# A hybrid decoder layer on one core: the prompt's mLSTM state kept over convolved inputs, a product moved to GpSimd, masks announced by halves

## The chip, the cores and the metric
The kernel runs on one core of one Trainium2 chip. The metric is the device time of one execution in microseconds, and the median of the runs counts.

## What is computed
One layer for a prompt of 1024 tokens and for 8 sample tokens that carry states: an input projection, a causal convolution, an SSD scan (16 heads) and an mLSTM scan (4 heads of 256) over chunks of 128 tokens, an output projection with a layer norm, and a product-key expert layer (PEER) that gathers 128 rows of u and v per token. The part that the change touches is the mLSTM of the prompt, with u_c the convolved input:

```
q = u_c @ w_mq;  k = u_c @ w_mk * DK**-0.5          # per head, 256 x 256
att = (q k^T) * exp(dmat - m_t);  num = att @ v + w_inter * (q @ c);  den = att.sum + w_inter * (q @ n)
c_new = w_old * c + (w_s * k)^T v;   n_new = w_old * n + (w_s * k).sum
```

The prompt begins with zero states, and c and n after the last chunk are outputs (p_c, p_n).

## The kernel before
Everything is in one program with semaphores set by hand; each engine has its own written-out order. There are three stages with a barrier between them.

1. **Projections** (to 559 us): TensorE makes channels and tokens from x in split precision, GpSimd splits the weights (L549, L551), VectorE convolves (L633, L635). ScalarE stores token products in DRAM (tok_d, L496) and waits at the end of the stage for all stores, s_ts among them.
2. **Scan** (560 to 856 us, `build_scan`): eight chunks. In each, TensorE transposes the chunk's rows and channels (L978 to L985), makes k and then q from cht and the weights wmk and wmq (L995), transposes k (L1002), makes the scores (L1007), turns the previous chunk's mix (L829), and does the intra-chunk SSD product (L1017: L by xdt), the products with the SSD state (L1024, L1034), one sample's row (L970), q by the state cst (L1043), attention by v (L1049) and the new state (L1053, L1057). ScalarE copies cols, btok and xtok (L1113 to L1115), takes exponentials of L head by head (L1138) with the copies of kT (at head 2) and qT (at head 10) between them. GpSimd adds the causal mask to L (L789), makes e_de and e_ws (L1208, L1209), dx (L1215), xdec (L1218), og (L1221) and scales hT (L1223). VectorE ends the previous chunk with its head norm (L796 to L808), the scaling (L811) and the mix (L814, L816), and then does xdt (L1273), kw (L1276) and the two halves of L by the score mask (L1279). While VectorE works on its norm, ScalarE takes the root in two small activations (L821, L823). Two samples' states are worked in beside it.
   SyncE's loads stand in one queue: v, states and, behind the previous mix, zo; then rows and rb of the next chunk, and cht once L1024 has read the old one. At the end ScalarE stores p_c and p_n, the last mixT, and mixs, the samples' mix, and waits for all of them.
3. **Experts** (856 us to the end, `build_peer`): 656 slots t, with one gathered row of u per slot on VectorE (L2009), rows of v 20 slots later on TensorE (L2388), and the norms, scores and picks of later token tiles spread over the slots by hand. Scores of the first tile are copied by ScalarE (L2120); VectorE picks from them in slots 1 to 22.

The rotating pair of PSUM views is `two(b)`, banks b and b+1. `free(engine, semaphore, n)` is a wait for n that is left out at n = 0.

Of the kernel before, what the change touches and what calls it, by code (L numbers as in the profile page):

```python
# [7 lines left out]
P = 128  # L8
D = 1024
KD = D // P  # L10
SEQ = 1024
CH = 128
# [76 lines left out]
def build(nc, a, o):  # L89
# [13 lines left out]
    mixt_d = dram("mixt_d", (NPAD // CH, P, 16, CH))  # L103
    bc_d = dram("bc_d", (NSMP, 4, P))
# [3 lines left out]
    with top:  # L108
# [19 lines left out]
        s_pre = nc.alloc_semaphore(name="scan_preloaded")  # L128
        with ExitStack() as ctx:
# [85 lines left out]
            s_ts = [sem(f"tok_stored{i}") for i in range(6)]  # L215
# [16 lines left out]
            with nc.Block() as block:  # L232
# [188 lines left out]
                def _(act):  # L421
# [113 lines left out]
                    for b in range(6):  # L535
                        act.wait_ge(s_ts[b], 16 * 3 * NTB // 2)
# [149 lines left out]
        with ExitStack() as ctx:  # L686
            build_scan(nc, a, o, ctx, sem, PB, ident, two, wo, s_wo, s_pre, pre, wp0, first, wp_d, cht_d, chs_d, ych_d, tok_d, rows_d, rows_s_d, mixt_d)
# [9 lines left out]
def build_scan(nc, a, o, ctx, sem, PB, ident, two, wo, s_wo, s_pre, pre, wp0, first, wp_d, cht_d, chs_d, ych_d, tok_d, rows_d, rows_s_d, mixt_d):  # L697
# [24 lines left out]
    qT, kT = sb("qT", [P, MH * KT, CH]), sb("kT", [P, MH * KT, CH])  # L722
# [5 lines left out]
    def wide(ap, n):  # L728
# [14 lines left out]
    hT, cst, nst = sb("hT", [P, D]), sb("cst", [P, MH * KT, DK + 1]), sb("nst", [P, MH * KT])  # L743
    ysb, yst, sq, og = (sb(n, [P, D]) for n in ("ysb", "yst", "sq", "og"))
# [20 lines left out]
    mte, x1e, _, g1e, b1e = first  # L765

    s = {n: sem("scan_" + n) for n in (
        "w wqk setup mask rows ch rb v zo pe_a pe_b pe_bk act_k pe_kk pe_st pe_tr pe_y pe_ys pe_hn pe_ni pe_nx pe_c1 pe_c2 "
        "act_xt act_small act_l act_qk act_l2 act_mt act_nx pool_l pool_arg pool_xdec pool_dx pool_hs pool_og "
        "dve_xdt dve_kw dve_mm dve_att dve_y dve_ys dve_h dve_num dve_var act_ln act_rs dve_c1 dve_c2 dve_mix "  # L770
        "outs stored passed mt0 x0 mt1 wp0 mix0").split()}
    ss = {n: sem("smp_" + n) for n in (
        "ld zeroed pad z_turned y2 ysum yvar yln yrs qk qkr qkt qkc exp arg nst cur outer c_new num numc den den_kept var ln rs mix turned kept stored").split()}
# [5 lines left out]
    def gate_y(ch, r, z, y):  # L779

        ch.link(V.tensor_tensor(y, y, z, ALU.mult))
        V.tensor_tensor_reduce(out=sq[0:r, :], in0=y, in1=y, scale=1.0 / D, scalar=EPS,
# [70 lines left out]
    with nc.Block() as block:  # L853
        @block.sync
        def _(sp):
            for i, q in pairs():
# [6 lines left out]
                if i == 0:  # L863
# [4 lines left out]
                    sp.sem_inc(s["wqk"], 32)  # L868
# [17 lines left out]
                free(sp, s["pe_c2"], i)  # L886
                for j in range(2):
# [53 lines left out]
        def _(pe):  # L941
# [31 lines left out]

            for i, q in pairs():
# [13 lines left out]
                if i == 0:  # L988
                    pe.wait_ge(s["setup"], 1)
                    pe.wait_ge(s["wqk"], 32)  # L990
# [1552 lines left out]
```

## Time and profile before

| | |
|---|---|
| median of 3 runs | 3362.64 us (3362.37 to 3376.76) |
| profiled execution | 3381.35 us, span 3379.5 us |
| mean granted TensorE clock | 0.969 of full |
| busy, share of the span | TensorE 92%, VectorE 75%, GpSimd 51%, ScalarE 28% |
| the scan stage | 560.4 to 855.98 us, chunks of about 31.6 us |
| HBM | 978.59 MB read, 93.11 MB written |

Durations below come from the profiled execution. Durations of TensorE overlap, so its pitch is read from one start to the next. An entry with "x8" sums eight instructions.

### The profile page before, as it was taken

The page shows a single profiled execution, that of the slowest core. Times are in us where ns is not written, and L with a number is a line of the kernel's source. Part 1 is how long each engine was busy: PE and PEld are TensorE (multiplying, and loading weights), DVE is VectorE, ACT ScalarE, POOL GpSimd, SP SyncE. Part 2 cuts the span into 40 slices and gives each one's busy share as a digit, 9 for nine tenths or more (in the row PEclk, how much of TensorE's full clock was granted, in tenths as well). Part 3 has the DMA queues.
Part 4 walks back from the last instruction along what each step waited for, and adds up shares of the span by engine and source line. Part 5 has one row for each costly group of instructions (what it writes and reads, how often), then busy time and mean ns, then how long its engine had stood idle before and what let it go on. Part 6 is the DMA issues. An engine that isn't in the chain of part 4 may idle for free.

```text
span 3379.5 us, 42480 instructions
## 1 busy us (share of the span) xinstructions
PE 3094.6 (92%) x13799; PEld 2052.6 (61%) x13799; DVE 2544.3 (75%) x5370; ACT 937.0 (28%) x2145; POOL 1709.5 (51%) x1418
## 2 busy tenths in 40 slices
PE   9999998999888888988877658999999999999998
PEld 9998887887333233322244336777677766677775
DVE  7771053887678888898899977777777777777777
ACT  3122222655011121111288771111111111111112
POOL 3232131442136666676654555555555555555554
PEclk9999999999999999999989789999999999999999
DMA  4435465778669999999989899999999999999997
GB/s 152 105 84 185 167 211 211 242 260 314 210 204 355 376 360 355 364 374 364 349 315 352 337 361 390 393 384 396 376 406 396 370 383 381 390 399 388 393 394 271
DMA packets 388784, 1074.52 MB, mean 318 GB/s; under 512 B 58824, under 2 KB 148744, under 8 KB 382176
## 3 DMA queue, kind: packets, MB, share of 16 engines
q0 software_dynamic: 186624, 679.56, 53.3%
q1 hardware_dynamic: 151280, 311.91, 26.0%
q10 hardware_dynamic: 50672, 80.51, 6.5%
q8 instruction: 102, 1.67, 0.2%
q14 instruction: 106, 0.87, 0.1%
HBM read 978.59 MB, written 93.11 MB: 317 GB/s over the span
## 4 chain that ended last, share of the span: by engine, by line
PE 40%; DVE 12%; DMA 9%; issue 8%; POOL 4%; ACT 1%; another core or an unknown queue 0%; POOLq 0%; DVEq 0%; SPq 0%; ACTq 0%; PEldq 0%
PE PB L2361 18%; PE PB L2348 14%; DMA vbf<-in_peer_v,gixv 4%; DVE ub L2009 4%; PE PB L2337 3%; DMA x1d<-in_peer_u 3%; PE PB L2388 2%; PE PB L2324 2%; POOL vbf L1737 2%; POOL ub L1737 2%; DMA ub<-in_peer_u,gix 1%; DVE ohb L1956 1%; PE PB L2306 1%; DVE oha L1954 1%; DMA vbf<-in_peer_v,gix 1%
## 5 line engine op out<-in xcount | busy, mean ns | idle before, releaser
L1737 POOL DMA_INDIRECT ub<-in_peer_u,gix x640 | 693.9, 1084 | 713.2 <-DVE hid L2009 507.6
L2361 PE MATMUL PB<-vbd,wd 128*128 128x512 f32 x1536 | 682.6, 594 | 0.0
L2348 PE MATMUL PB<-xds,uts 128*128 128x384 f32 x3072 | 569.4, 340 | 0.0
L2348 PEld LDWEIGHTS PB<-xds,uts 128*128 128x128 f32 x3072 | 531.7, 189 | 0.5 <-issue 0.5
L1737 POOL DMA_INDIRECT vbf<-in_peer_v,gix x340 | 398.6, 1172 | 160.5 <-issue 100.6
L2361 PEld LDWEIGHTS PB<-vbd,wd 128*128 128x128 f32 x1536 | 283.2, 191 | 308.1 <-issue 308.1
L2388 PE MATMUL PB<-vbf,dg 128*64 128x512 f32 x1200 | 320.7, 658 | 113.1 <-DMA vbf<-in_peer_v,gixv 94.5
L1737 POOL DMA_INDIRECT vbf<-in_peer_v,gixv x300 | 323.2, 1077 | 172.5 <-issue 88.5
L1970 DVE TENSOR_TENSOR uts<-PB,uts 128x512 fp32r<-128x512 f32 x256 | 175.6, 686 | 295.7 <-ACT uts L2183 284.0
L2009 DVE CUSTOM_DVE_ANT_0 ub<-ub,x1g 128x1024 f32<-128x1024 f32 x257 | 313.0, 1221 | 51.5 <-DMA ub<-in_peer_u,gix 33.0
L2183 ACT CAST uts<-PB 128x512 fp32r<-128x512 f32 x256 | 149.9, 586 | 642.0 <-PE PB L2337 594.6
L2009 DVE CUSTOM_DVE_ANT_0 ub<-ub,x1gb 128x1024 f32<-128x1024 f32 x256 | 313.0, 1223 | 5.2 <-DMA ub<-in_peer_u,gix 5.0
L2050 DVE SCALAR_TENSOR_TENSOR acc<-vbf,wg,acc 128x1024 f32<-128x1024 f32 x212 | 271.1, 1279 | 5.9 <-DMA vbf<-in_peer_v,gix 4.6
L2388 PEld LDWEIGHTS PB<-vbf,dg 128*64 128x64 f32 x1200 | 85.6, 147 | 298.3 <-issue 272.0
L2306 PE MATMUL PB<-wo,mt 128*128 128x512 f32 x512 | 243.2, 619 | 15.2 <-DVE x L1800 14.8
L2324 PE MATMUL PB<-wp,x1T 128*128 128x512 f32 x432 | 198.6, 602 | 0.0
L2306 PEld LDWEIGHTS PB<-wo,mt 128*128 128x128 f32 x512 | 95.6, 196 | 162.8 <-issue 162.8
L2188 ACT ACTIVATE hg<-PB 128x384 f32<-128x384 f32 x128 | 62.7, 490 | 465.2 <-PE PB L2348 465.2
L2432 PE MATMUL PB<-oha,ohb 128*128 128x128 f32 x768 | 119.1, 309 | 78.7 <-DVE ohb L1956 61.1
L2009 DVE CUSTOM_DVE_ANT_0 ub<-ub,acc 128x1024 f32<-128x1024 f32 x128 | 155.3, 1225 | 32.9 <-DMA ub<-in_peer_u,gix 17.1
L2432 PEld LDWEIGHTS PB<-oha,ohb 128*128 128x128 f32 x768 | 106.0, 214 | 118.8 <-DVE ohb L1956 87.7
L2213 ACT ACTIVATE dg<-fold,wgv 128x64 f32<-128x64 f32 x300 | 87.5, 340 | 324.7 <-PE PB L2388 169.3
(427 smaller groups left out, 5099.0 us busy)
## 6 DMA issues: line engine op xcount, KB each, us to landing
vbd<-in_peer_v SPq DMA_DIRECT2D x128, 512.0 KB
x1d<-in_peer_u SPq DMA_DIRECT2D x96, 512.0 KB
gd_d<-stag ACTq DMA_DIRECT2D x12, 2048.0 KB
gbd<-gd_d SPq DMA_DIRECT2D x16, 1536.0 KB
ubd<-in_peer_u SPq DMA_DIRECT2D x32, 512.0 KB
wtr<-in_w_tok SPq DMA_DIRECT2D x6, 2048.0 KB
tok_d<-stg ACTq DMA_DIRECT2D x48, 256.0 KB, 2.0
rb_e<-rows_d SPq DMA_DIRECT2D x8, 1536.0 KB, 10.5
```

The lines of the kernel that those rows point to most:

```text
L1737: pool.indirect_dma_start(out=buf, out_offset=None, in_=a[table], in_offset=bass.IndirectOffsetOnAxis(ap=index, axis=0)).then_inc(done, 16)
L1970: V.tensor_tensor(uts[:, b % 2, 1, 4 * x:4 * x + 4, :].rearrange("p k e -> p (k e)"), PB[:, 7, :], uts[:, b % 2, 0, 4 * x:4 * x + 4, :].re ...
L2009: V.tensor_tensor_reduce(out=ub[:, t % NB, :], in0=ub[:, t % NB, :], in1=by, scale=1.0, scalar=0.0, op0=ALU.mult, op1=ALU.add, accum_out=i ...
L2050: V.scalar_tensor_tensor(y, vbf[:, v % NB, :], wg[:, hv % 2, col:col + 1], y, ALU.mult, ALU.add, accum_out=total).then_inc(s["ax"], 1)
L2183: S.copy(uts[:, b % 2, 0, 4 * x:4 * x + 4, :].rearrange("p k e -> p (k e)"), PB[:, 7, :]).then_inc(s["utc"], 1)
L2306: last = T.matmul(PB[:, 2 + h, :], mt[:, m % 2, j % 4, :], wo[:, j, h * 512:(h + 1) * 512], start=j == 0, stop=j == 15)
L2324: last = T.matmul(PB[:, 4 + n, :].rearrange("p (h n) -> p h n", h=4), x1T[:, kk, :], wp[:, 4 * n:4 * n + 4, kk, :] if n else wp0[:, :, kk, :],
L2337: last = T.transpose(PB[:, 7, j * P:(j + 1) * P], ubd[b % 4][:, (4 * x + j) * P:(4 * x + j + 1) * P], ident[:, :])
L2348: last = T.matmul(PB[:, 6, 0:TD], uts[:, b % 2, ul, k, :], xds[:, xl, k, :], start=(k, n) == (0, 0), stop=(k, n) == (KD - 1, 2))
L2361: last = T.matmul(PB[:, 2 * d + n, :], wd[:, b % 2, d * CH:(d + 1) * CH], vbd[b % 8][:, n * 512:(n + 1) * 512], start=b == 0, stop=b == NB ...
L2388: last = T.matmul(PB[64 * g:64 * g + 64, x, :], dg[:, n % 2, g, :], vbf[:, (v0 + g) % NB, x * 512:(x + 1) * 512], start=v0 % CH == 0, stop ...
L2432: last = T.matmul(PB[:, 2 + m % 2, :].rearrange("p (b t) -> p b t", t=4)[:, :, x], ohb[:, m % 2, x, :], oha[:, m % 2, x, :], start=True, s ...
```

## The change
For the prompt, the keys are no longer made. Before chunk 0 TensorE turns both weights (32 transposes), and makes per head the product of w_mk and w_mq over their inner dimension, which VectorE keeps with the factor DK**-0.5 in mu0 and mu1. In each chunk one product with it takes the place of the q and k products; its result is scored against the convolved inputs themselves (cht), these are transposed instead of kT, and the state cst is kept over them. The final state (with its sum column) is stored as it is in cu_d; in slots 3 and 6 of the expert stage TensorE multiplies it by w_mk, ScalarE scales it in slots 5 and 7 and stores p_c and p_n, and the first gather of v waits for these stores. Besides: xdt is made by GpSimd, ahead of dx and xdec; exponentials and masks of L are announced by halves; VectorE's memsets are in another order; token stores are awaited by those who need them in the scan, and the mixs store by the first v index loads of the expert stage. The scratch tiles sq, kT and nst are gone.

```diff
+    cu_d = dram("cu_d", (P, MH * KT, DK + 1))
...
+        def tokens_stored(eng):
+
+            for b in range(6):
+                eng.wait_ge(s_ts[b], 16 * 3 * NTB // 2)
+
...
-                    for b in range(6):
-                        act.wait_ge(s_ts[b], 16 * 3 * NTB // 2)
...
+                if i == 0:
+                    tokens_stored(sp)
...
+            def weight_product(h):
+                pe.wait_ge(s["wk_kept"], h + 1)
+                pe.wait_ge(s["wq_kept"], h + 1)
+                for d in range(KT):
+                    for e in range(KT):
+                        last = T.matmul(PB[:, 4 + h, d * DK:(d + 1) * DK], wqT[:, h, e, d * P:(d + 1) * P], wkT[:, h, e, :],
+                                        start=e == 0, stop=e == KT - 1)
+                last.then_inc(s["m_made"], 1)
+
+            pe.wait_ge(s_pre, 80)
+            for h in range(MH):
+                for w, bank in ((wmk, 4 + h), (wmq, h)):
+                    for k in range(KT):
+                        for e in range(KT):
+                            last = T.transpose(PB[:, bank, e * DK + k * P:e * DK + (k + 1) * P], w[:, h, k, e * P:(e + 1) * P], ident[:, :])
+                    last.then_inc(s["w_turned"], 1)
+            weight_product(0)
+            weight_product(1)
+            pe.wait_ge(s["wq_kept"], MH)
...
                 if i == 0:
-                    pe.wait_ge(s["setup"], 1)
-                    pe.wait_ge(s["wqk"], 32)
-                for w, b, done in ((wmk, 6, "pe_bk"), (wmq, 4, "pe_b")):
-                    for h in range(MH):
-                        for e in range(KT):
-                            for k in range(KT):
-                                last = T.matmul(two(b)[:, (h * KT + e) * CH:(h * KT + e + 1) * CH],
-                                                w[:, h, k, e * P:(e + 1) * P], cht[:, UT0 + h * KT + k, :],
-                                                start=k == 0, stop=k == KT - 1)
-                    last.then_inc(s[done], 1)
-                pe.wait_ge(s["act_k"], i + 1)
+                    weight_product(2)
+                    weight_product(3)
+                for h in range(MH):
+                    if i == 0:
+                        pe.wait_ge(s["m_kept"], h + 1)
+                    for e in range(KT):
+                        for k in range(KT):
+                            last = T.matmul(two(4)[:, (h * KT + e) * CH:(h * KT + e + 1) * CH],
+                                            mu(h)[:, k, e * P:(e + 1) * P], cht[:, UT0 + h * KT + k, :],
+                                            start=k == 0, stop=k == KT - 1)
+                last.then_inc(s["pe_b"], 1)
+                pe.wait_ge(s["act_xt"], i + 1)
                 pe.sem_inc(s["passed"], 1)
                 for j in range(MH * KT):
-                    last = T.transpose(two(0)[:, j * P:(j + 1) * P], kT[:, j, :], ident[:, :])
+                    last = T.transpose(two(0)[:, j * P:(j + 1) * P], cht[:, UT0 + j, :], ident[:, :])
...
-                        last = T.matmul(PB[:, 2, h * CH:(h + 1) * CH], kT[:, h * KT + k, :], qT[:, h * KT + k, :],
+                        last = T.matmul(PB[:, 2, h * CH:(h + 1) * CH], cht[:, UT0 + h * KT + k, :], qT[:, h * KT + k, :],
...
-                pe.wait_ge(s["dve_mm"], i + 1)
                 pe.wait_ge(s["dve_kw"], i + 1)
+                pe.wait_ge(s["pool_xdt"], i + 1)
                 for h in range(NH):
+                    if h % 8 == 0:
+                        pe.wait_ge(s["dve_mm"], 2 * i + h // 8 + 1)
...
                     if h == 2:
-                        act.wait_ge(s["pe_bk"], i + 1)
-                        free(act, s["pe_st"], i)
-                        S.activation(kT[:, :, :].rearrange("p a n -> p (a n)"), two(6), ACT.Copy, scale=DK ** -0.5).then_inc(s["act_k"], 1)
-                    if h == 10:
                         act.wait_ge(s["pe_b"], i + 1)
                         free(act, s["pe_nx"], i)
                         S.copy(qT[:, :, :].rearrange("p a n -> p (a n)"), two(4)).then_inc(s["act_qk"], 1)
...
-                last.then_inc(s["act_l"], 1)
+                    if h % 8 == 7:
+                        last.then_inc(s["act_l"], 1)
...
-            S.copy(nst[:, :].unsqueeze(2), cst[:, :, DK:DK + 1]).then_inc(ss["nst"], 1)
-            act.dma_start(o["p_c"], cst[:, :, 0:DK]).then_inc(s["outs"], 16)
-            act.wait_ge(ss["nst"], 1)
-            act.dma_start(o["p_n"], nst[:, :]).then_inc(s["outs"], 16)
+            act.dma_start(cu_d, cst[:, :, :]).then_inc(s["outs"], 16)
...
-            act.wait_ge(ss["stored"], 16)
...
-                    pool.wait_ge(s["setup"], 1)
-                pool.wait_ge(s["dve_xdt"], i + 1)
+                free(pool, s["pe_y"], i)
+                G.tensor_tensor(heads(xdt[:, :], HD), heads(xtok[:, :], HD), wide(cols[q][:, R_DT:R_DT + NH], HD), ALU.mult).then_inc(s["pool_xdt"], 1)
                 free(pool, s["dve_y"], i)
                 G.tensor_tensor(heads(dx[:, :], HD), heads(xtok[:, :], HD), wide(dsk[:, :], HD), ALU.mult).then_inc(s["pool_dx"], 1)
                 pool.wait_ge(s["act_small"], i + 1)
+                pool.wait_ge(s["pool_xdt"], i + 1)
...
+            def keep_turned(h):
+                dve.wait_ge(s["w_turned"], 2 * h + 1)
+                V.tensor_copy(wkT[:, h, :, :].rearrange("p e d -> p (e d)"), PB[:, 4 + h, :]).then_inc(s["wk_kept"], 1)
+
+            def keep_product(h):
+                dve.wait_ge(s["m_made"], h + 1)
+                V.tensor_scalar(mu(h).rearrange("p k e -> p (k e)"), PB[:, 4 + h, :], DK ** -0.5, None, ALU.mult).then_inc(s["m_kept"], 1)
...
-                dve.wait_ge(s["act_xt"], i + 1)
-                free(dve, s["pe_y"], i)
-                free(dve, s["pool_xdec"], i)
-                V.tensor_tensor(heads(xdt[:, :], HD), heads(xtok[:, :], HD), wide(cols[q][:, R_DT:R_DT + NH], HD), ALU.mult).then_inc(s["dve_xdt"], 1)
...
-                dve.wait_ge(s["act_l"], i + 1)
                 for g in range(NG):
-                    last = V.tensor_tensor(L[:, g * 8:g * 8 + 8, :], L[:, g * 8:g * 8 + 8, :],
-                                           PB[:, 3, g * CH:(g + 1) * CH].unsqueeze(1).to_broadcast([P, 8, CH]), ALU.mult)
-                last.then_inc(s["dve_mm"], 1)
+                    dve.wait_ge(s["act_l"], 2 * i + g + 1)
+                    V.tensor_tensor(L[:, g * 8:g * 8 + 8, :], L[:, g * 8:g * 8 + 8, :],
+                                    PB[:, 3, g * CH:(g + 1) * CH].unsqueeze(1).to_broadcast([P, 8, CH]), ALU.mult).then_inc(s["dve_mm"], 1)
...
                 def load_first_gixv(part):
+                    if part == 0:
+                        sp.wait_ge(s_mixs, 16)
...
                 load_mt(2, 0)
+                sp.wait_ge(s["iota"], 1)
+                for n in range(2):
+                    sp.dma_start(wk[n], a["w_mk"][:, 2 * n:2 * n + 2, :, :]).then_inc(s["cul"], 16)
+                sp.dma_start(cu, cu_d).then_inc(s["cul"], 16)
...
                 def gather_v(v):
+                    if v == 0:
+                        pool.wait_ge(s["c_out"], 32)
...
+                    if t in (5, 7):
+                        n = (t - 5) // 2
+                        act.wait_ge(s["c_made"], n + 1)
+                        for b in range(2):
+                            S.activation(cu[:, 4 * n + 2 * b:4 * n + 2 * b + 2, :], PB[:, 4 * b:4 * b + 2, 0:DK + 1], ACT.Copy, scale=DK ** -0.5).then_inc(s["c_kept"], 1)
+                        if n:
+                            act.wait_ge(s["c_kept"], 4)
+                            act.dma_start(o["p_c"], cu[:, :, 0:DK]).then_inc(s["c_out"], 16)
+                            S.copy(nu.unsqueeze(2), cu[:, :, DK:DK + 1]).then_inc(s["c_kept"], 1)
+                            act.wait_ge(s["c_kept"], 5)
+                            act.dma_start(o["p_n"], nu).then_inc(s["c_out"], 16)
...
+                    if t in (3, 6):
+                        n = t // 6
+                        if n == 0:
+                            pe.wait_ge(s["cul"], 48)
+                            pe.wait_ge(s["scc"], 2)
+                        else:
+                            pe.wait_ge(s["c_kept"], 2)
+                        for j in range(4):
+                            h, e, bank = 2 * n + j // 2, j % 2, (0, 1, 4, 5)[j]
+                            for k in range(KT):
+                                last = T.matmul(PB[:, bank, 0:DK + 1], wk[n][:, j // 2, k, e * P:(e + 1) * P], cu[:, h * KT + k, :],
+                                                start=k == 0, stop=k == KT - 1)
+                        last.then_inc(s["c_made"], 1)
+                    if t == 9:
+                        pe.wait_ge(s["c_kept"], 4)
```

## Rows read from the trace of the kernel before

**Rows 1.** Busy time in two stretches; columns: stretch, length, busy (instructions), PEclk, DMA share, GB/s.
```profile
599.70:789.40 189.70, 186.25 (x1388) 158.66 (x1387) 162.69 (x243) 119.66 (x326) 86.59 (x43) 1.00 0.77 265
892.00:2460.00 1568.00, 1330.71 (x4866) 688.24 (x4865) 1318.13 (x3605) 484.39 (x1195) 933.85 (x850) 0.94 0.95 353
```

**Rows 2.** Timeline of chunk 3, all engines: start, duration, engine, line, output<-inputs.
```profile
662.94 0.26 PE L978 MATMUL PB<-ident,rows_e 48*128 48x48 f32 x1
...
664.72 3.74 PE L995 MATMUL PB<-cht_e,wmk_e 128*128 128x128 f32 x32
...
666.58 0.20 POOL L1209 TENSOR_TENSOR e_ws<-cols,rb_e 128x4 f32<-128x4 f32 x1
...
666.85 0.17 DVE L803 TENSOR_TENSOR rs<-mv,den 128x4 f32<-128x4 f32 x1
...
667.74 0.17 DVE L808 TENSOR_TENSOR rs<-rs,den 128x4 f32<-128x4 f32 x1 [0.51 <-ACT rs L823]
...
668.29 3.74 PE L995 MATMUL PB<-cht_e,wmq_e 128*128 128x128 f32 x32
...
669.41 2.44 ACT L1138 ACTIVATE L<-L,cols 128x128 f32<-128x128 f32 x8
670.56 1.22 DVE L816 TENSOR_TENSOR mix<-num,og 128x1024 f32<-128x1024 f32 x1
671.69 1.22 DVE L1273 TENSOR_TENSOR xdt<-xtok,cols 128x1024 f32<-128x1024 f32 x1
...
672.99 1.90 POOL L1215 TENSOR_TENSOR dx<-xtok,dsk 128x1024 f32<-128x1024 f32 x1 [6.21 <-DVE xdt L1273]
...
674.87 2.35 DVE L1279 TENSOR_TENSOR L<-L,PB 128x1024 f32<-128x1024 f32 x2 [0.63 <-ACT L L1138]
...
675.02 1.91 PE L829 MATMUL PB<-ident,mix 128*128 128x128 f32 x16
...
677.28 3.79 PE L1017 MATMUL PB<-xdt,L 128*128 128x64 f32 x32 [0.34 <-DVE L L1279]
...
685.58 3.64 PE L1043 MATMUL PB<-cst,qT 128*128 128x257 f32 x16
...
694.55 0.26 PE L978 MATMUL PB<-ident,rows_e 48*128 48x48 f32 x1
```

**Rows 3.** Timeline of the first stage, VectorE and GpSimd working at once.
```profile
229.09 4.07 POOL L549 CAST wtkh<-wtr 128x4096 fp32r<-128x4096 f32 x1
...
229.61 3.57 DVE L633 TENSOR_SCALAR cv<-xps,cw 128x8 f32<-128x8 f32 x1
...
233.22 10.12 DVE L635 SCALAR_TENSOR_TENSOR cv<-xp,cw,cv 128x1024 f32<-128x1024 f32 x1
233.24 9.02 POOL L551 TENSOR_TENSOR wtkl<-wtr,wtkh 128x4096 fp32r<-128x4096 f32 x1
```

**Rows 4.** Busy time of TensorE just ahead of the scan; columns as named.
```profile
559.00:560.00 1.00, 0.00 (x0) 0.57 0.00 0
```

**Rows 5.** Timeline from the end of the first stage into chunk 0.
```profile
556.53 0.33 ACTq L496 DMA_DIRECT2D tok_d<-stg  x1
...
560.42 0.31 PE L978 MATMUL PB<-ident,rows_e 48*128 48x48 f32 x1 [4.56 <-SPq L865]
...
565.75 5.56 PE L995 MATMUL PB<-cht_e,wmk_e 128*128 128x128 f32 x32 [1.84 <-DVE v L1235]
...
575.98 2.05 PE L1007 MATMUL PB<-qT,kT 128*128 128x128 f32 x16 [0.23 <-ACT qT L1137]
```

**Rows 6.** Timeline at the end of the scan stage.
```profile
835.39 17.33 PE L1065 MATMUL PB<-wo,mt 128*128 128x512 f32 x40
...
843.41 1.08 ACTq L1190 DMA_DIRECT2D mixt_d<-mixs  x1
...
855.98 1.28 ACT L2124 ACT_TABLE_LOAD   x1 [12.60 <-PEq L118]
```

**Rows 7.** Busy time early in the expert stage; columns as in rows 1.
```profile
920.00:930.00 10.00, 3.14 (x4) 1.51 (x5) 9.52 (x40) 0.00 (x0) 2.81 (x3) 0.55 0.54 157
```

More of the change, by code:

```diff
@@ L128, in build @@
         s_pre = nc.alloc_semaphore(name="scan_preloaded")
+        s_ts = [nc.alloc_semaphore(name=f"tok_stored{i}") for i in range(6)]
+        s_mixs = nc.alloc_semaphore(name="smp_mix_stored")
+        def tokens_stored(eng):
+            for b in range(6):
+                eng.wait_ge(s_ts[b], 16 * 3 * NTB // 2)
         with ExitStack() as ctx:
@@ L686, in build @@
         with ExitStack() as ctx:
-            build_scan(nc, a, o, ctx, sem, PB, ident, two, wo, s_wo, s_pre, pre, wp0, first, wp_d, cht_d, chs_d, ych_d, tok_d, rows_d, rows_s_d, mixt_d)
+            build_scan(nc, a, o, ctx, sem, PB, ident, two, wo, s_wo, s_pre, pre, wp0, first, wp_d, cht_d, chs_d, ych_d, tok_d, rows_d, rows_s_d, mixt_d, cu_d, tokens_stored, s_mixs)
         end_phase()
@@ L694, in pairs, with build_scan @@
         yield i, i % 2
-def build_scan(nc, a, o, ctx, sem, PB, ident, two, wo, s_wo, s_pre, pre, wp0, first, wp_d, cht_d, chs_d, ych_d, tok_d, rows_d, rows_s_d, mixt_d):
+def build_scan(nc, a, o, ctx, sem, PB, ident, two, wo, s_wo, s_pre, pre, wp0, first, wp_d, cht_d, chs_d, ych_d, tok_d, rows_d, rows_s_d, mixt_d, cu_d, tokens_stored, s_mixs):
     f32 = mybir.dt.float32
@@ L742, in build_scan @@
     kw = sb("kw", [P, D])
[L743 to L744 removed]
+    hT, cst = sb("hT", [P, D]), sb("cst", [P, MH * KT, DK + 1])
+    ysb, yst, mu1, og = sb("ysb", [P, D]), sb("yst", [P, D]), sb("mu1", [P, 2, KT, DK]), sb("og", [P, D])
     nx, num = sb("nx", [P, MH, DK + 1]), sb("num", [P, MH, DK + 1])
@@ L781, in gate_y @@
         ch.link(V.tensor_tensor(y, y, z, ALU.mult))
-        V.tensor_tensor_reduce(out=sq[0:r, :], in0=y, in1=y, scale=1.0 / D, scalar=EPS,
+        V.tensor_tensor_reduce(out=yst[0:r, :], in0=y, in1=y, scale=1.0 / D, scalar=EPS,
                                op0=ALU.mult, op1=ALU.add, accum_out=rs[0:r, 0:1])
@@ L1086, in _ @@
         def _(act):
+            for h in range(MH):
+                act.wait_ge(s["w_turned"], 2 * h + 2)
+                S.copy(wqT[:, h, :, :].rearrange("p e d -> p (e d)"), PB[:, h, :]).then_inc(s["wq_kept"], 1)
             S.preload_act_table_set("natural_log_exp_and_others")
@@ L1189, in _ @@
             act.wait_ge(ss["pad"], 16)
-            act.dma_start(mixt_d[NCH, :, :, 0:B], mixs[:, :, :], allow_slow_non_contiguous=True).then_inc(ss["stored"], 16)
-            act.wait_ge(s["outs"], 64)
+            act.dma_start(mixt_d[NCH, :, :, 0:B], mixs[:, :, :], allow_slow_non_contiguous=True).then_inc(s_mixs, 16)
+            act.wait_ge(s["outs"], 48)
             for q in range(2):
@@ L1359, in build_peer @@
     mt, x1, x1T, gb1, gb2 = L_["first"]
-    mixt_d, wp_d = (L_[k] for k in ("mixt_d", "wp_d"))
+    mixt_d, wp_d, cu_d = (L_[k] for k in ("mixt_d", "wp_d", "cu_d"))
+    s_mixs = L_["s_mixs"]
     V, S, T = nc.vector, nc.scalar, nc.tensor
@@ L1654, in _ @@
                     if t == 64:
+                        sp.wait_ge(s["c_made"], 2)
                         load_gix(1)
```

47 lines of the change are left out of this document (31 added, 16 removed).

## Prediction

> **What bounds the kernel now.** I read the stages first. In chunks 1 to 6 of the scan TensorE is busy for 186.25 of 189.70 us, VectorE for 162.69 and GpSimd for 86.59; in the long expert stage no engine is full, but the DMA engines are at 0.95 and move 353 GB/s [rows 1]. The change touches the scan's loop, its two edges and eight slots of the expert stage, so what counts is the scan's loop, and there the order of work on TensorE.
>
> The timeline of chunk 3 shows that loop [rows 2]. It runs from 662.94 to 694.55: 31.61 us. TensorE transposes the chunk's inputs, makes k (L995, wmk: 664.72 to 668.29, 3.57 us at its pitch), makes q (3.57 more), does transposes and scores, turns the previous chunk's output at 675.02 and begins the intra-chunk product (L1017) at 677.28, once VectorE has masked both halves of L (L1279: 674.87 + 2.35 = 677.22). Everything behind L1017 keeps its distance from it, to the next chunk. So the change is worth, per chunk, what it does to the start of L1017. Two inputs can set that start: TensorE's own queue, and VectorE's chain of head norm, mix (L816, done 671.78), xdt, kw, mask. In the kernel before they come out almost together.
>
> **The loop, if nothing collides.** Removed on TensorE: the k product, 3.57 us. The k copy on ScalarE goes too, so the q copy takes its place, and the scores can start 3.57 us earlier, with the chunk's transposes already done behind the product. Removed on VectorE: xdt, 1.22 us. TensorE would turn the mix as soon as it is there, at 671.8 instead of 675.02. VectorE would do kw from 671.8 (1.2, the length of xdt beside it) and half a mask (2.35 / 2 = 1.18): 674.2. ScalarE's exponentials don't hold this: eight take 2.44 us, and the first eight follow the q copy, so they end at about 671.4, 3 us before the first masked half is wanted. L1017 starts at 674.2 instead of 677.28: 3.1 us per chunk gained.
>
> **What collides.** xdt moves to GpSimd, in front of dx and xdec, and no longer waits for VectorE. In the kernel before dx waited 6.21 us for VectorE's xdt and started at 672.99, after the mix. Now the three run from where e_ws ends, 666.58 + 0.20 = 666.8: a product of this shape takes 1.90 us (dx), xdec has the same shape, and xdt too. So GpSimd is busy from 666.8 to 672.5, over just that part of VectorE's head norm that runs from L803 (666.85) to the end of L816 (671.78). That overlap doesn't exist in the kernel before; the first stage shows what it costs [rows 3]. There VectorE's product with a scalar on 8 elements per partition, started at 229.61, lasts 3.57 us, to the end of GpSimd's cast (229.09 + 4.07 = 233.16); its next instruction, two SBUF inputs, started at 233.22, lasts 10.12 us, and GpSimd's product beside it runs from 233.24 to 242.26. VectorE stood still while GpSimd worked, and got through one small instruction between two of GpSimd's. And it is fair: the cast, asked for at 229.09, took its turn ahead of that small instruction although VectorE had it next in line.
>
> Applied here: L803, issued just after xdt starts, ends with xdt at 668.7. L804, which needs L803, ends with dx at 670.6. ScalarE's two small activations for the root stand between L804 and L808 and take about the 0.7 us that lie between L803 and L808 less the small instruction, so L808 is issued at about 671.2 and ends with xdec at 672.6. From L808 to the end of L816 it is 671.78 - 667.74 = 4.04 us: the mix is done at 676.5, 4.7 us later than before. Then kw and half a mask, 2.4 us: L1017 starts at 678.9 to 679.0 against 677.28. The same comes out if L803 slips in first, for L808 and the scalings behind it then meet the later two of GpSimd's. TensorE waits for the mix before its transposes, where it has 16 to do in 1.91 us, and these fit beside kw and the mask. So the k product that TensorE saves turns into a wait for VectorE: 1.7 us per chunk lost. SyncE's load of zo stands behind the mix and is late with it, and rows and rb of the next chunk are queued behind zo; I take them as hidden, since zo is read behind L1017 and the others at the next chunk's start. The masks by halves are worth the 1.18 us that this already contains.
>
> It happens for chunks 1 to 7; chunk 0 has no head norm before it and the last norm has no GpSimd work beside it. Term one: 7 x 1.7 = +11.9 us. Bounds: with no collision 7 x -3.1 = -21.7; if VectorE kept its turn once it had it, only two of the three would be waited for, 1.9 less: -0.2 per chunk, -1.4.
>
> The Trainium skill (SBUF — State Buffer, section "SBUF: two separate sides") says the same as a rule: a VectorE instruction with two SBUF inputs, or in a two-port mode, and one of GpSimd take one port pair in turns, whoever starts first, for the whole instruction. Rows 3 agree, with 3.57 and 10.12 us. By that rule the term is +11.9; without it, it would be -21.7. It speaks against moving work between just these two engines.
>
> **Chunk 0.** Added on TensorE: 32 transposes, at 1.91 / 16 = 0.12 us: 3.8 us; four weight products of 8 passes over 256 columns, at 3.64 / 16 = 0.23 us (257 columns): 7.3 us. Removed: the k product, and the wait for VectorE's memsets (1.84 idle) [rows 5]. The wait for the token stores leaves the stage's edge; ScalarE issues the last one until 556.86 and TensorE starts at 560.42, and I take 1.2 us off, between 0 and 2. From 559.2, 3.8 + 7.3 + 1.8 (chunk inputs, 664.72 - 662.94) + 3.6 (q) and 1.25 for the copy to the scores make 576.9, plus some 0.4 of small waits: 577.3 against 575.98 now, +1.3. The clock adds to it: just before the stage, with TensorE idle, the granted clock reads 0.57 [rows 4], and the k product took 5.56 us where it takes 3.74 in chunk 3, so the front of the stage ran at 1.2 GHz, half of full. If the new transposes run so too for some 3 to 5 us, they lose 1.5 to 2.5. Term two: +3.2, between +1 and +5.5. The evacuations of turned weights (eight copies of 512 columns, on ScalarE and VectorE) lie beside the transposes and products; uncovered they would cost a few tenths each.
>
> **The scan's end.** The mixs store, issued from 843.41, is no longer waited for at the barrier; TensorE's last product ends at 852.72 and the next stage starts at 855.98 [rows 6]. Term three: -1, between 0 and -2. The 1 MB store of p_c becomes one of cu_d; nothing else changes in bytes.
>
> **The expert stage.** Added: 2 x 8 passes per slot in slots 3 and 6, 3.64 us of TensorE; four scaled copies on ScalarE and two stores; 2.1 MB loaded and 1 MB stored. At 920 to 930 TensorE is busy for 3.14 of 10 us, ScalarE for 0 and DMA for 0.54, while VectorE has 9.52 [rows 7]: it bounds these slots, and gets nothing new. ScalarE waits for slot 3's product behind the first scores, so the next score copy is late, but VectorE picks from it only in slot 8. On SyncE the loads stand ahead of gixv, which is wanted after slot 16. Gathers of v begin behind the two stores, in slot 21. Term four: 0. If this cover failed, 3.1 MB at 353 GB/s [rows 1] would be 8.9 us.
>
> **Sum.** +11.9 + 3.2 - 1 + 0 = +14.1 us on the profiled execution's 3381.35 us (span 3379.5): 3395.5. That execution lies 18.7 us above the median of 3362.64; on the median it gives **3376.7 us**, 0.4% slower.
>
> **Rivals.**
> - *No collision* (the change does all that it says): -21.7 + 3.2 - 1 = -19.5, 3343 us, 0.6% faster. For it: the saving on TensorE is certain, and VectorE would fit under it. Against it: rows 3. It decides if the mix (L816) ends at under 9 us from the chunk's start. Chance 0.12.
> - *Half a collision*: VectorE keeps its turn for the scalings and the mix while xdec waits: -1.4 + 3.2 - 1 = +0.8, 3363 us. Against it: the cast in rows 3 got its turn between two of VectorE's. Chance 0.15.
> - *The collision and the expert stage too*: the loads and stores come in where DMA bounds: +14.1 + 8.9 = +23, 3386 us. Against it: DMA at 0.54 in those slots. Chance 0.10.
> - The forecast: 0.60; 0.03 is left for what I don't see.
>
> **Range and chances.** The range holds the forecast with its terms' bounds (7 x 1.4 + 1 - 2 = +9 to 7 x 2 + 5.5 = +19.5) and half a collision down to -6, and stops short of no collision and of the far end of the third rival: 3356 to 3384 us. About 0.5%, 17 us, is what a measurement of this kernel can tell from no change. Faster by more than that: 0.12 (no collision). Slower by more: the third rival and a quarter of the forecast, 0.26. The rest, 0.62, within.
>
> **What would show it.** In chunks 1 to 7: GpSimd's xdt starting some 3.9 us after the chunk's first transpose; L803 and L804 at nearly 1.9 us each instead of 0.17; the mix ending some 13.5 us after the chunk's start instead of 8.8; TensorE idle ahead of the mix transposes by 1.5 to 2 us; chunks of 33.3 us. Wrong if these instructions keep their 0.17 us, or if chunks come out at 28.5 us. In chunk 0 the scores start at 577 to 580. In the expert stage, the first dot of chunk 1 is reached as long after 855.98's counterpart as before, or term four is wrong.

## The result and the profile after

The changed kernel took 3387.77 us (median of 17 runs, 3376.55 to 3398.54) against 3367.84 us of the kernel before beside it (17 runs, 3355.55 to 3376.76). The ratio is 1.006, 95% interval 1.0048 to 1.0072: about 20 us slower (16 to 24). Slower was foreseen, by the collision between GpSimd and VectorE, but 14.1 us of it; and the 3362.64 us that the forecast stood on was 5.2 us under the 3367.84 found in more runs. The measured time lies above the range of 3356 to 3384.

The profiled execution (3382.85 us, span 3381.0) shows the loop in its windows, which answer to [rows 1]; the columns are the same. Chunks 1 to 6 take 201.48 us instead of 189.70. TensorE has less to do (176.60 instead of 186.25), VectorE is busy longer (175.34 instead of 162.69) with fewer instructions, and the granted clock is 0.93 instead of 1.00. The long expert stage has much the same busy times.

```profile
600.65:802.13 201.48, 176.60 (x1196) 148.23 (x1195) 175.34 (x237) 112.78 (x320) 99.22 (x49) 0.93 0.71 249
907.00:2475.00 1568.00, 1354.54 (x4980) 708.38 (x4979) 1331.91 (x3625) 490.29 (x1207) 948.95 (x858) 0.95 0.96 359
```

The timeline of chunk 3 answers to [rows 2]. Lines have moved: L815, L816, L828, L841, L1053 are the L803, L804, L816, L829, L1017 of before, and L1041 is L1007.

```profile
669.07 0.26 PE L1011 MATMUL PB<-ident,rows_e 48*128 48x48 f32 x1
...
670.85 3.74 PE L1029 MATMUL PB<-cht_e,mu 128*128 128x128 f32 x32
...
672.86 1.90 POOL L1246 TENSOR_TENSOR xdt<-xtok,cols 128x1024 f32<-128x1024 f32 x1
672.98 1.80 DVE L815 TENSOR_TENSOR rs<-mv,den 128x4 f32<-128x4 f32 x1
...
674.72 1.90 POOL L1248 TENSOR_TENSOR dx<-xtok,dsk 128x1024 f32<-128x1024 f32 x1
674.82 1.83 DVE L816 TENSOR_SCALAR rs<-rs 128x4 f32<-128x4 f32 x1
...
676.68 0.21 ACT L833 ACTIVATE rs<-rs 128x5 f32<-128x5 f32 x1 [3.39 <-DVE rs L816]
...
677.17 1.34 DVE L820 TENSOR_TENSOR rs<-rs,den 128x4 f32<-128x4 f32 x1 [0.52 <-ACT rs L835]
...
678.66 3.16 PE L1041 MATMUL PB<-qT,cht_e 128*128 128x128 f32 x16 [3.20 <-ACT qT L1173]
...
681.16 1.22 DVE L828 TENSOR_TENSOR mix<-num,og 128x1024 f32<-128x1024 f32 x1
...
682.43 3.68 PE L841 MATMUL PB<-ident,mix 128*128 128x128 f32 x16 [0.61 <-DVE mix L828]
...
685.90 3.83 PE L1053 MATMUL PB<-xdt,L 128*128 128x64 f32 x32
```

Here the reader sees the collision as forecast: L815 and L816, 0.17 us each before, take 1.80 and 1.83 and end with GpSimd's xdt and dx; L820 takes 1.34; the mix is done at 682.38, 13.3 us after the chunk's start (foreseen: 13.5). What was not foreseen stands on TensorE. ScalarE sits for 3.39 us in front of the root (L833), q's copy is queued behind it, and so TensorE waits 3.20 us ahead of the scores, not ahead of the mix. Behind that wait the scores take 3.16 us instead of 2.05 (their length in the kernel before), and the sixteen transposes of the mix take 3.68 us instead of 1.91 [rows 2]: TensorE runs at 1.2 GHz, half of 2.4. L1053 starts 16.83 us after the chunk's start and has no wait of its own: TensorE is late, half the mask was ready at 684.6 (VectorE's mask starts at 683.43 and takes 2.34, and half of that is 1.17).

The same kernel shows what the clock costs. Its chunks 1 to 3 take 34.2 us, its chunks 4 to 6 take 32.97, although the same 3.20 us wait stands in all of them. In chunks 4 and 6 the clock falls too, but is back by the time of the mix's transposes (2.11 and 1.97 us); in chunk 5 it doesn't fall:

```profile
745.79 2.05 PE L1041 MATMUL PB<-qT,cht_e 128*128 128x128 f32 x16 [3.20 <-ACT qT L1173]
749.56 1.97 PE L841 MATMUL PB<-ident,mix 128*128 128x128 f32 x16 [1.72 <-DVE mix L828]
751.91 3.76 PE L1053 MATMUL PB<-xdt,L 128*128 128x64 f32 x32 [0.39 <-DVE L L1326]
```

So VectorE's chain alone makes a chunk 1.36 us longer than before's 31.61, and the lower clock adds another 1.2 where it lasts through the transposes of the mix.

Chunks 0 and 7 answer to [rows 5] and [rows 6].

```profile
558.09 0.63 PE L1001 MATMUL PB<-ident,wmk_e 128*128 128x128 f32 x4 [2.90 <-PEq L119]
...
575.24 2.05 PE L1041 MATMUL PB<-qT,cht_e 128*128 128x128 f32 x16 [0.23 <-ACT qT L1173]
...
589.91 5.40 PE L1080 MATMUL PB<-cst,qT 128*128 128x257 f32 x16 [2.33 <-DVE rsy L1351]
...
850.70 17.33 PE L1102 MATMUL PB<-wo,mt 128*128 128x512 f32 x40
...
871.26 1.28 ACT L2184 ACT_TABLE_LOAD   x1 [17.00 <-PEq L119]
```

The front of the scan ran at full clock in this execution, L1080 did not (5.40 us; 3.64 in the loop, and 3.72 at the same place in the kernel before, behind the same wait of 2.33), and the next stage starts 15.3 us later than before (871.26 - 855.98).

### The profile page after: what moved, and what is told of

The parts are those of the page before. It is cut to its first block, busy times and chain, and to the rows that moved or that the text cites. A ratio compares the mean times of both kernels' runs of the same rounds, so it can differ in the third digit from the quotient of the medians.

```text
span 3381.0 us, 42161 instructions
## 1 busy us (share of the span) xinstructions
PE 3095.9 (92%) x13639; PEld 2051.3 (61%) x13639; DVE 2560.4 (76%) x5370; ACT 932.9 (28%) x2145; POOL 1728.6 (51%) x1426
## 4 chain that ended last, share of the span: by engine, by line
PE 41%; DVE 12%; DMA 11%; issue 6%; POOL 2%; ACT 1%; DVEq 0%; SPq 0%; POOLq 0%; ACTq 0%; PEldq 0%
PE PB L2432 17%; PE PB L2419 13%; DMA x1d<-in_peer_u 4%; DVE ub L2069 4%; PE PB L2395 3%; DMA vbf<-in_peer_v,gixv 3%; PE PB L2408 3%; PE PB L2459 3%; DMA ub<-in_peer_u,gix 3%; POOL vbf L1795 1%; DVE ohb L2016 1%; POOL ub L1795 1%; PE PB L2377 1%; PE PB L2518 1%; DVE oha L2014 1%
## 5 line engine op out<-in xcount | busy, mean ns | idle before, releaser
L2069 DVE CUSTOM_DVE_ANT_0 ub<-ub,acc 128x1024 f32<-128x1024 f32 x128 | 155.4, 1226 | 23.4 <-DMA ub<-in_peer_u,gix 15.1
```

The costliest lines, as they stand in the source:

```text
L2069: V.tensor_tensor_reduce(out=ub[:, t % NB, :], in0=ub[:, t % NB, :], in1=by, scale=1.0, scalar=0.0, op0=ALU.mult, op1=ALU.add, accum_out=i ...
```

## The experiments

Every kernel was run beside the kernel before on the same chip, and a ratio is to that. The table puts beside it, from each one's profile, where chunk 1 starts (before: 599.71), how long chunks 1 to 6 take (before: 189.7) and by how much the expert stage starts later than before's 855.98 (its first table load).

| kernel | ratio, 95% interval | chunk 1 | chunks 1 to 6 | stage start |
|---|---|---|---|---|
| changed kernel | 1.0060 (1.0048 to 1.0072) | 600.65 | 201.5 | +15.3 |
| changed kernel again | 1.0067 (1.0042 to 1.0092) | 603.26 | 202.7 | +19.8 |
| xdt back on VectorE | 0.9994 (0.9978 to 1.0010) | 602.32 | 186.5 | -2.0 |
| GpSimd's products behind the mix | 0.9973 (0.9956 to 0.9990) | 602.34 | 176.4 | -12.4 |
| the same again | 0.9973 (0.9957 to 0.9989) | 602.41 | 178.0 | -10.7 |
| spare product on TensorE | 1.0074 (1.0054 to 1.0093) | 603.63 | 199.7 | +16.6 |
| no turning | 1.0063 (1.0041 to 1.0086) | 602.48 | 204.8 | +21.0 |
| before, xdt on GpSimd | 1.0069 (1.0047 to 1.0091) | 599.34 | 207.6 | +23.6 |
| before, xdt on GpSimd behind the mix | 1.0006 (0.9993 to 1.0019) | 602.59 | 189.7 | +3.6 |
| behind the mix, whole masks | 1.0051 (1.0032 to 1.0071) | 605.78 | 202.2 | +19.1 |
| behind the mix, no turning | 0.9968 (0.9952 to 0.9985) | 601.47 | 176.4 | -12.8 |
| root behind q | 1.0075 (1.0057 to 1.0093) | 602.32 | 205.2 | +20.9 |

The last column accounts for the ratios (0.1% is 3.4 us), within their intervals in all rows but two, the changed kernel and the spare product, where it falls 1 to 2 us short of them: within a few us, what a kernel gains or loses is made before the expert stage starts. One profile can be off by some 3 us: the kernel before with xdt behind the mix has before's chunks to 0.01 us, and 2.9 of its +3.6 come from chunk 0.

**xdt back on VectorE.** Changed kernel, xdt computed behind the mix on VectorE; GpSimd waits for it as before.

```diff
-                G.tensor_tensor(heads(xdt[:, :], HD), ...)  # GpSimd, ahead of dx
+                V.tensor_tensor(heads(xdt[:, :], HD), ...)  # VectorE, ahead of kw
```

> The changed kernel with one edit undone: xdt is made by VectorE again, after the mix. Theory (VectorE and GpSimd take turns at a memory port, and xdt, dx and xdec on GpSimd stand over VectorE's head norm): L815 and L816 go back from 1.8 us to 0.17 us, the mix ends 8.8 us after the chunk's start instead of 13.3, L1053's counterpart starts at 12.5 instead of 16.8 and chunks last 29.7 us instead of 33.6: 27 us under the changed kernel, about 7 us under the kernel before. Rival (the chunks are longer because VectorE's and ScalarE's order has changed with the keys gone, and not through xdt): chunks stay above 33 us, no more than 3 us gained.

Ratio 0.9994, so the move of xdt, which also lets dx and xdec start earlier, makes a change that would be neutral into one that costs 0.66%. Three of its chunks take 29.6 to 29.9 us and chunk 3 takes 31.4; chunks 1 and 6 take 32.9 and 33.0, and the timeline shows why. The same wait stands ahead of L1053 in all six, but in two of them the product behind it runs at half clock:

```profile
738.56 3.76 PE L1053 MATMUL PB<-xdt,L 128*128 128x64 f32 x32 [1.52 <-DVE L L1328]
...
768.19 5.43 PE L1053 MATMUL PB<-xdt,L 128*128 128x64 f32 x32 [1.52 <-DVE L L1328]
...
773.42 3.62 PE L1061 MATMUL PB<-hT,cht_e 128*128 128x512 f32 x4
```

That is 1.67 + 1.68 us more (L1061 takes 1.94 elsewhere), the whole 3.3 between the two kinds of chunk. The chunks at full clock have the 29.7 us expected. The two others, and chunk 3, where TensorE waits 1.58 us for a sample's sum, are why the kernel comes out at before's time and not 7 us under it.

**GpSimd's products behind the mix.** One wait ahead of xdt in GpSimd's queue.

```diff
+                free(pool, s["dve_mix"], i)
                 free(pool, s["pe_y"], i)
                 G.tensor_tensor(heads(xdt[:, :], HD), ...)
```

> The changed kernel with GpSimd's xdt, dx and xdec held until VectorE has written the previous chunk's mix; all else as changed. Theory: the same three products on the same engine, but no longer beside the head norm, so that this keeps its old length; chunks last 28.5 us, up to 29.5 if the sample's state addition, which now meets xdec, comes late for TensorE; 29 to 35 us under the changed kernel, 10 to 16 under the kernel before. Rival (GpSimd is simply too slow for xdt, 1.90 us against 1.22): holding it back makes it later still, and the chunks come out longer than 33.6 us.

> The changed kernel with GpSimd's three products released by the mix, once more and on another chip: in the first its ratio to before was 0.9973, and its chunks took 28.84 us but for one of 31.98. Theory A: again 0.995 to 0.999, with five of six chunks at 28.8 us and the next stage's first product 12 us ahead of before's. Rival B (the two profiled scans of this code that ended early were fortunate): chunks of 32 us in most places and a ratio above 0.999.

Both runs give 0.9973: faster than both kernels, 0.87% under the changed one. Its chunk 3:

```profile
663.93 0.17 DVE L815 TENSOR_TENSOR rs<-mv,den 128x4 f32<-128x4 f32 x1
664.13 0.17 DVE L816 TENSOR_SCALAR rs<-rs 128x4 f32<-128x4 f32 x1
...
668.77 1.22 DVE L1324 TENSOR_TENSOR kw<-PB,e_ws 128x1024 f32<-128x1024 f32 x1
...
668.93 1.90 POOL L1247 TENSOR_TENSOR xdt<-xtok,cols 128x1024 f32<-128x1024 f32 x1 [5.08 <-DVE mix L828]
...
671.26 3.76 PE L1053 MATMUL PB<-xdt,L 128*128 128x64 f32 x32 [0.39 <-DVE L L1327]
...
672.76 3.94 DVE L1307 TENSOR_TENSOR cs<-cs,t4s 128x2048 f32<-128x2048 f32 x1
...
676.63 2.39 DVE L1340 TENSOR_TENSOR ych<-ych,rsy 128x64 f32<-128x64 f32 x1
...
682.94 3.72 PE L1080 MATMUL PB<-cst,qT 128*128 128x257 f32 x16 [3.12 <-DVE numr L1314]
```

The small operations are back at 0.17, and L1053 starts 11.25 us after the chunk's start (660.01), where the rival without a collision had put it: 11.3 (674.2 - 662.94). Four of the six chunks take 28.8 us and chunk 4 takes 29.1, in both runs. kw, which reads PSUM, runs at its 1.22 us beside xdt; the sum into cs, with two SBUF inputs, takes 3.94 (2.29 in the changed kernel, 4.36 before) beside GpSimd's xdec and og, and TensorE doesn't wait for it. In chunk 3 VectorE has two more small operations behind it (L1340 and L1341: 2.39 and 1.82 us beside og and the scaling of hT, 0.21 and 0.22 before), and TensorE waits 3.12 us for a sum behind them. In the second run L1080 ran at half clock behind this wait, 5.40 us, and that chunk took 33.66 instead of 31.98.

**The kernel before with xdt on GpSimd, at either place.** k's product, whole masks and all stores stay.

```diff
+                free(pool, s["dve_mix"], i)      # only in the second of the two
+                free(pool, s["pe_y"], i)
+                G.tensor_tensor(heads(xdt[:, :], HD), ...)
...
-                V.tensor_tensor(heads(xdt[:, :], HD), ...)
```

> The kernel before with one edit: xdt is computed on GpSimd ahead of dx and xdec, as in the changed kernel; k's product, whole masks and all stores stay. Theory A (GpSimd's three products over VectorE's head norm are the loss): the two small VectorE operations ahead of the root take about 1.8 us each instead of 0.17, the mix is ready 3 us later in a chunk, q's copy is late only by what the root holds ScalarE, and the chunk is 1.5 to 4 us longer, since this one has k's product to run as well: the kernel is 10 to 30 us slower than before. Rival B (xdt's removal from VectorE pays for it): within 5 us of before. Rival C (the loss comes from the shorter TensorE work, so that it idles and its clock falls): without that, no more than 5 us slower.

> The kernel before with xdt on GpSimd (as in the run that was 1.0069 of before), but with GpSimd's three products released by the mix instead of by the copy of x. Theory A (the place of GpSimd's work is the loss, not GpSimd's 1.90 us for 1.22 on VectorE): the head norm's two small operations are back at 0.17 us, and the chunk is back at 31.6 us or a little under, since VectorE has one operation of 1.22 us less: 0.997 to 1.001 of before. Rival B (a product on GpSimd late in the chunk delays y's product or the later products): 1.003 and more.

1.0069 and 1.0006. The one move, without anything else of the change, costs as much as the whole change did; with the same work released by the mix it costs nothing that can be measured. The clock is not what costs in the first: chunks 3 to 6 have a granted clock of 1.00 and still take 34.27 us, 2.7 more than before; in chunks 1 and 2, where it fell, it is 3.7. Nor is it the shorter work of TensorE, for k's product is there. In the first, the VectorE rows of the collision are those of the changed kernel, and y's product (L1018) waits for the mask, 16.99 us after the chunk's start at 669.90, against 14.34 before. Most of what lies between this and 15.73, where the kernel with the spare product below starts it behind the same collision, is the whole mask in place of halves:

```profile
673.69 1.90 POOL L1215 TENSOR_TENSOR xdt<-xtok,cols 128x1024 f32<-128x1024 f32 x1
673.82 1.80 DVE L803 TENSOR_TENSOR rs<-mv,den 128x4 f32<-128x4 f32 x1
...
682.73 2.05 PE L1007 MATMUL PB<-qT,kT 128*128 128x128 f32 x16 [2.08 <-ACT qT L1138]
...
686.89 3.79 PE L1018 MATMUL PB<-xdt,L 128*128 128x64 f32 x32 [0.35 <-DVE L L1278]
```

**A spare product on TensorE.** Changed kernel, with 32 unused passes ahead of k's transposes, as long as the product that the change removed.

```diff
+                for h in range(MH):
+                    for e in range(KT):
+                        for k in range(KT):
+                            T.matmul(two(6)[:, ...], mu(h)[:, k, e * P:(e + 1) * P], ...)
```

> The changed kernel with TensorE doing a second, unused product of the same size as the one for q (32 passes, 3.57 us, into two banks that nothing reads) in each chunk, where the k product was. Theory (part of the loss comes from TensorE's clock, which fell to half after it had waited 3.2 us for the q copy): TensorE waits less, the mix is turned at full clock in 1.9 us and not 3.7, L1053 starts 15.7 us after the chunk's start and not 16.8, chunks last about 32.5 us, 7 to 8 us under the changed kernel although it does more work. Rival (only the wait for the mix counts): chunks stay at 33.6 us, no change.

The clock stays at 1.00, and the chunk has the price of VectorE's chain alone: five of six take 32.97 us, 1.36 over the 31.61 of before and the same as the changed kernel's chunks 4 to 6, with TensorE waiting ahead of the mix and ahead of L1059 (the L1053 of the others), which starts 15.73 us after the chunk's start (669.57).

```profile
674.93 3.74 PE L1036 MATMUL PB<-cht_e,mu 128*128 128x128 f32 x32
...
682.94 1.97 PE L841 MATMUL PB<-ident,mix 128*128 128x128 f32 x16 [1.62 <-DVE mix L828]
685.30 3.76 PE L1059 MATMUL PB<-xdt,L 128*128 128x64 f32 x32 [0.39 <-DVE L L1332]
```

The kernel as a whole is not faster: the 7 to 8 us expected were too much. Chunks 1 to 6 take 199.7 us, 1.8 of them in chunk 3, where TensorE waits 1.59 us for a sample's sum. The three executions of the changed scan (two here, one in the kernel without turning) take 201.5, 202.7 and 204.8, and the last of them has that wait as well. Six chunks of 32.97 are 197.8; beyond that, and beyond the 1.8 in the last, the lower clock cost 3.7, 4.9 and 5.2 us, some 4.6 on average and less than the ratios can tell: it fell into three, four and four of the six chunks for long enough to count.

**The root behind q's copy.** The rival that the late q is the loss.

```diff
-                if i:
-                    root(act, P, i - 1)
                 act.wait_ge(s["pool_l"], i + 1)
...
                         S.copy(qT[:, :, :]..., two(4)).then_inc(s["act_qk"], 1)
+                        if i:
+                            root(act, P, i - 1)
```

> The changed kernel with ScalarE's two operations of the root (L833, L835) behind the copy of q instead of ahead of the masks' exponentials. Theory A (VectorE sets the chunk, 32.97 us by its own chain, and the late q adds to it only by the idle time ahead of the scores, behind which TensorE's clock falls and the mix's transposes take 3.68 us instead of 1.97): the scores start 3 us earlier in a chunk, the idle time moves ahead of the mix's transposes, 4 to 5 us in one piece, the transposes or y's product still run at half clock in most chunks, and the chunk stays between 33 and 35 us: within 6 us of the changed kernel (ratio 1.004 to 1.008). Rival B (the late q is the loss): the chunks fall to 32 us or less, the kernel comes within 5 us of before.

1.0075, no better. The scores start 6.62 us after the chunk's start instead of 9.59, and the wait is now one piece ahead of the mix, with half a clock behind it as well:

```profile
677.77 2.05 PE L1041 MATMUL PB<-qT,cht_e 128*128 128x128 f32 x16 [0.23 <-ACT qT L1171]
...
684.52 3.21 PE L841 MATMUL PB<-ident,mix 128*128 128x128 f32 x16 [4.70 <-DVE mix L828]
```

**Whole masks, behind the mix.** The halves undone in the fastest kernel.

```diff
-                    if h % 8 == 0:
-                        pe.wait_ge(s["dve_mm"], 2 * i + h // 8 + 1)
+                pe.wait_ge(s["dve_mm"], i + 1)
...
-                    dve.wait_ge(s["act_l"], 2 * i + g + 1)
+                    if g == 0:
+                        dve.wait_ge(s["act_l"], 2 * i + 2)
```

> The kernel with GpSimd's three products behind the mix, and in it one thing undone: the masks are announced whole, so that TensorE waits for both halves ahead of y's product. Theory A (in that kernel the wait ahead of y's product is for the mask's first half, 0.39 us idle, and the second half ends about 1 us later): the idle time is 1.4 us instead, as in the kernel with xdt back on VectorE, and in some chunks the clock falls behind it, which cost that kernel 3.3 us in each of two chunks: 8 to 18 us slower than with halves (0.9973 of before), so 0.9995 to 1.003 of before. Rival B (later waits take the idle time back, as the wait for the sample's sum in chunk 3 does): within 3 us of the kernel with halves.

1.0051 instead of 0.9973: some 26 us, more than the 8 to 18 expected. The wait ahead of y's product is 2.34 us, since the first half now waits for ScalarE's second eight exponentials too, and in five of six chunks the clock falls in it (chunk 3):

```profile
685.54 2.35 DVE L1327 TENSOR_TENSOR L<-L,PB 128x1024 f32<-128x1024 f32 x2 [0.73 <-ACT L L1173]
...
688.04 4.77 PE L1052 MATMUL PB<-xdt,L 128*128 128x64 f32 x32 [2.34 <-DVE L L1327]
...
692.60 3.73 PE L1060 MATMUL PB<-hT,cht_e 128*128 128x512 f32 x4
```

Chunks take 33.7 us on average instead of 29.4. Chunk 4, behind a wait of 2.08 us, stays at full clock and takes 30.45, 1.4 over its 29.1 with halves; that is the price of the longer wait. The other five take 33.7 to 35.3: 3.3 to 4.9 us more, by the clock. So most of the loss is the clock.

**No turning.** The state and its normaliser are not multiplied by w_mk in slots 3 and 6, and the loads, copies and stores that go with it are left out, once in the changed kernel and once in the fastest.

```diff
-                    if t in (3, 6):
+                    if t in ():
```

> The changed kernel without the turning of the state by w_mk in the expert stage: no loads of w_mk and cu, no products, copies or stores there; p_c is stored unturned at the end of the scan and p_n is not stored. Theory (the turn costs about 5 us: what is left of the 20 us measured after the 15.3 us that the scan lost, 3.1 MB in a stage where DMA is the bound): 4 to 9 us under the changed kernel. Rival (the slots hide it, as forecast, but for the 1.5 us by which the first slots are late): 0 to 2 us under it.

> The kernel with GpSimd's three products behind the mix, without the turning of the state in the expert stage (the state and its normaliser leave the scan unturned and the normaliser is not stored: this part of the computation is left out). Theory A (the transfers that the turning adds to a stage bound by the DMA engines take their time there, 3.1 MB at 353 GB/s, 8.9 us at most): 4 to 9 us under the kernel with the turning (0.9973 of before), so 0.9946 to 0.9961. Rival B (the stage takes them up, as the first pair of kernels without and with it suggested, where both were 1.006 of before but the one without had the longer scan by 5 us in its profile): 0.996 to 0.998.

1.0063 beside 1.0060 and 1.0067 with it, 0.9968 beside 0.9973 twice: the turning costs nothing that can be measured; some 6 us would still fit into the intervals. The prediction's own sign agrees: the first dot of the second token tile (chunk 1 of the expert stage) comes 467.5 us after the stage's start in the kernel before, 463.5 and 458.1 in the changed kernel, and 467.4 and 456.5 in the two without turning. It scatters by more than 10 us, and not with the turning.

**The changed kernel again.**

> The changed kernel once more, beside the run of the kernel before on this chip. In the two profiled executions of its scan so far (its own and that of the kernel without the turning, whose scan code is the same) the last chunk started at 802.1 and 807.3 us against 789.4 before, so the scan alone gives +13 to +18 at that point, some +15 to +20 at its end. Theory A (the whole difference is made in the scan): the ratio is again 1.004 to 1.007, and the next stage's first product comes 15 to 21 us later than before in the profile, however much later the run is as a whole. Rival B (the expert stage adds some 5 us of its own): the ratio is the same, but the scan's delay stays at 15 and the measured difference above 20.

The same ratio, and a stage start of +19.8 us instead of +15.3. With the kernel without turning, whose scan is the same code, there are three executions of the changed scan: +15.3, +19.8, +21.0, on average 18.7, within the 16 to 24 us measured. The expert stage needs no share, though one of a few us is not ruled out.

## Why the prediction was right in its cause and too low in its size

- **The collision** (term one): right. L803 and L804 at nearly 1.9 us: 1.80 and 1.83. Mix after 13.5 us: 13.3. The Trainium skill's rule (SBUF — State Buffer, section "SBUF: two separate sides") held in both directions: L815 and L820, with two SBUF inputs, waited, and kw, with one of its two in PSUM, did not. L816, with one SBUF input, waited as well; by the rule it must have run in a two-port mode, which no trace here shows. The collision as the cause is shown by the two kernels before with xdt on GpSimd, 1.0069 and 1.0006.
- **The step that failed** is in term one: that TensorE would wait ahead of the mix, and that the transposes "fit beside kw and the mask". It left ScalarE's queue out: the root stands ahead of q's copy, so TensorE waited 3.20 us ahead of the scores; and it let every product behind a wait run at full clock. At full clock the chunk is 1.36 us longer (foreseen 1.7, so the VectorE part was a little too dear); with the clock down up to the transposes of the mix it is 2.6. Chunks 1 to 6 lost 11.8, 13.1 and 15.1 us in the three executions, on average 13.3, where 6 x 1.7 = 10.2 stood: 8.1 for VectorE's chain (197.8 less 189.7), 4.6 for the clock, and 0.6 for a wait for a sample's sum, 1.8 us that one of the three had. That the root's place is not itself the cost is shown by the kernel with the root behind q.
- **Chunk 0** (term two, +3.2): chunk 1 started 0.9, 3.5 and 2.8 us later. In the first, the new transposes ran at full clock (0.63 us for four), in the other two about the first fifteen at half, as assumed. But before's front varies as well: with it (before and its two variants) chunk 1 started at 599.71, 599.34 and 602.59, on average 600.55, against 602.13 with the new one. By that the term is +1.6. The sign given for it, scores at 577 to 580, missed in the profiled execution (575.24). In the same chunk q by the state (L1080) takes 5.3 to 5.4 us in all executions with the new front but one, and 3.72 in two of three with the old one; the prediction had no term for that.
- **The scan's end** (term three, -1): wrong, nothing was saved. From TensorE's last product to the next stage it is 3.23 us (871.26 - 868.03), as the 3.26 of before. From the start of chunk 7 to the next stage the three executions have 2.5 to 3.2 us more than before, of which chunk 7's own loss is 1.4 to 2.6. What makes the rest, up to 1.9, stays open.
- **The expert stage** (term four, 0): nothing speaks against it, by the two kernels without turning, within some 6 us.
- **The rivals.** "No collision" is what the kernel with the products behind the mix shows: chunks of 28.84 us, where 28.5 stood. It decides where the mix ends; here 8.9 us after the chunk's start. "Half a collision" falls with L815, L816 and L820, which waited for all three. "The collision and the expert stage too" came nearest in time, 3386 us, but for its second half no run shows anything: it was the clock and the base, not the expert stage. That its number fits is chance.

The sum by the average of the three: 2.4 + 13.3 + 3.0 = 18.7 where 3.2 + 10.2 + 0.7 = 14.1 stood. The forecast of 3376.7 us is 11.1 under the measured 3387.8: 4.6 of that are in this sum, 5.2 are the median of before, known from three runs only, and 1.3 lie between the traces' 18.7 and the measured 19.9, within its interval.

What stays open: why the same wait, of 1.52 us in one kernel and of 3.20 in another, drops the clock in one chunk and not in the next.

## What to carry to other kernels

Work moved from VectorE to GpSimd is priced by what VectorE does at that moment, not by GpSimd's idle time: in the kernel before, xdt on GpSimd cost 0.7% where the three products of 1.90 us stood over a chain of small operations with SBUF inputs, and nothing measurable where one wait put them behind the mix, beside kw and the mask, which read PSUM. In the changed kernel the same wait turned 0.6% slower than before into 0.3% faster. When a change frees an engine, follow the queues of all the others to see where it will wait next, and price what runs behind that wait at half clock as well. A mask announced by halves was worth 1.4 us in a chunk at full clock, somewhat over half its 2.35, and 4.9 to 6.5 where the longer wait was followed by half clock.

## What the runs showed of the hardware

A wait of TensorE as short as 1.52 us can be followed by half clock, with 5.43 us for a product that takes 3.76; the same wait in the same place left four of six chunks alone. In the kernel with whole masks, the wait of 2.34 us was followed by it in five of six chunks, and the sixth, at full clock, had one of 2.08; in the changed kernel, one of the six waits of 3.20 us was not. What a fall costs depends on what comes next: in chunks 4 and 6 of the changed kernel only the scores ran slower, ahead of a wait for VectorE, and the chunk lost nothing by it.

A VectorE operation on four elements per partition with SBUF inputs that starts during a GpSimd operation takes what is left of that one (1.80 us instead of 0.17), and GpSimd's next one starts as it ends, ahead of the next small one, so a chain of such operations moves by one per GpSimd product. kw, 1024 elements with one input in PSUM, takes 1.22 us with and without xdt beside it.
